# A two-group encoder layer on one core: GpSimd's order in the prompt attention, VectorE's order in the first sample step, and a split final step of the ConvFFN

## The reference, cut to what matters

```python
D_MODEL, SEQ, DEC_SEQ, PAST_LEN = 1024, 1024, 64, 2048      # one prompt, one running stream
SB_HEADS, SB_HEAD_DIM, GM_GROUPS, D_FF = 16, 64, 8, 2816

h = rms_norm(x, g_pre_mix)
u_a, v_a, q, k, v_b = split(h @ w_in)
y_a = gelu(u_a) * (tril(w_s) @ layer_norm(gelu(v_a)) + b_s)          # per group, 128-position chunks
# stick-breaking attention, strictly causal, in 128-query blocks:
z = q k^T / 8
after = exclusive reverse cumsum over keys of log_sigmoid(-z)
y_b = exp(log_sigmoid(z) + after) @ v_b
g_a, g_b = sigmoid(h @ w_gate + b_gate)
x = x + rms_norm((g_a * (y_a @ w_branch_a) + g_b * (y_b @ w_branch_b)) @ w_o, g_post_mix)
up = rms_norm(x, g_pre_ffn) @ w_up                                    # 1024 -> 2 x 2816
conv = b_conv + sum_i w_conv[i] * shifted(up, i)                      # causal, width 3
ff = (gelu(conv_gate) * conv_value) @ w_down
x = x + rms_norm(ff, g_post_ffn)
```

## Time and profile before

| | us |
|---|---|
| median of 3 runs | 2316.68 (2316.09 to 2316.88) |
| the profiled execution | 2319.07 |
| its span in the trace | 2317.3 |
| TensorE busy | 2167.2 (94%) |
| VectorE busy | 1317.6 (57%) |
| GpSimd busy | 921.4 (40%) |
| ScalarE busy | 746.1 (32%) |
| granted TensorE clock, mean | 0.973 |

### The profile page before, as it was taken

One profiled execution on the slowest core, in us unless ns is written; L12 is line 12 of the kernel. 1 busy time (PEld: TensorE's weight loads), 2 busy tenths in 40 slices (PEclk: granted clock), 3 DMA queues, 4 the chain that ended last, 5 costly groups with the idle time before them and its releaser, 6 DMA issues. The chain is left out here.

```text
span 2317.3 us, 33750 instructions
## 1 busy us (share of the span) xinstructions
PE 2167.2 (94%) x12884; PEld 2057.6 (89%) x12884; DVE 1317.6 (57%) x1715; ACT 746.1 (32%) x1435; POOL 921.4 (40%) x495
## 2 busy tenths in 40 slices
PE   6999999998898999989996989799999999999993
PEld 6999999998888999979996968799999999999992
DVE  5044120004777777856554557676776767667666
ACT  3222102225666766744332122212121121211212
POOL 2335334446655555547552210423324233242404
PEclk9999999999999999999997989899999999999996
DMA  5125324636544554565636342201111111111104
GB/s 171 46 78 178 119 76 135 170 125 164 147 113 111 140 131 122 136 186 145 183 105 197 112 163 87 87 28 55 39 43 48 34 54 36 45 45 36 45 0 165
DMA packets 290821, 237.40 MB, mean 102 GB/s; under 512 B 51142, under 2 KB 267926, under 8 KB 290710
## 3 DMA queue, kind: packets, MB, share of 16 engines
q1 hardware_dynamic: 281968, 222.24, 33.2%
q10 hardware_dynamic: 7510, 9.19, 1.3%
q0 software_dynamic: 1232, 4.46, 0.5%
HBM read 168.51 MB, written 67.33 MB: 102 GB/s over the span
## 5 line engine op out<-in xcount | busy, mean ns | idle before, releaser
L1131 DVE TENSOR_TENSOR_SCAN p_rest<-p_rest 128x896 f32<-128x896 f32 (+7 forms) x128 | 230.4, 1814 | 249.6 <-ACT p_rest L1064 249.2
L168 PE MATMUL p_psU<-mergedT_lo,p_w_hi 128*128 128x364 f32 x1056 | 347.0, 329 | 3.3 <-ACTq L2146 3.3
L170 PE MATMUL p_psU<-mergedT_hi,p_w_lo 128*128 128x364 f32 x1056 | 347.7, 329 | 0.0
L169 PE MATMUL p_psU<-mergedT_hi,p_w_hi 128*128 128x364 f32 x1056 | 347.3, 329 | 0.0
L148 POOL TENSOR_SCALAR p_w_hi<-p_w_raw 128x1024 fp32r<-128x1024 f32 x72 | 98.3, 1366 | 558.3 <-PE p_psD L170 417.4
L2169 DVE TENSOR_TENSOR p_acc<-p_psD,p_acc 128x512 f32<-128x512 f32 (+1 forms) x396 | 273.3, 691 | 45.3 <-PE p_psD L170 44.0
L282 PE MATMUL p_psB<-hT_lo,w_hi 128*128 128x364 f32 x888 | 295.6, 333 | 2.4 <-issue 2.4
L282 PE MATMUL p_psB<-hT_hi,w_lo 128*128 128x364 f32 x888 | 293.2, 330 | 0.0
L282 PE MATMUL p_psB<-hT_hi,w_hi 128*128 128x364 f32 x888 | 292.4, 329 | 0.0
L922 POOL TENSOR_TENSOR p_weights<-p_weights,p_rest 128x895 f32<-128x895 f32 (+7 forms) x128 | 171.1, 1348 | 184.2 <-DVE p_rest L1131 184.2
L168 PEld LDWEIGHTS p_psU<-mergedT_lo,p_w_hi 128*128 128x128 f32 x1056 | 199.2, 189 | 5.6 <-POOLq L132 3.4
(11 more groups left out here) (255 smaller groups left out, 4692.7 us busy)
## 6 DMA issues: line engine op xcount, KB each, us to landing
p_w_raw<-in_w_up SPq DMA_DIRECT2D x44, 512.0 KB, 3.7
w_raw<-in_w_in SPq DMA_DIRECT2D x40, 512.0 KB, 3.9
p_w_raw<-in_w_down SPq DMA_DIRECT2D x22, 512.0 KB, 3.5
p_kT<-k_hi_scratch SPq DMA_DIRECT2D x32, 256.0 KB, 4.7
p_kT<-k_lo_scratch SPq DMA_DIRECT2D x32, 256.0 KB, 5.2
w_raw<-in_w_gate SPq DMA_DIRECT2D x16, 512.0 KB, 4.0
p_raw_v<-in_cache_sb_v SPq DMA_DIRECT2D x8, 1024.0 KB, 6.1
p_raw_k<-in_cache_sb_k SPq DMA_DIRECT2D x7, 1024.0 KB, 6.4
```

What stands on the lines that cost most here:

```text
L168: nc.tensor.matmul(out, stat_hi, mov_lo, start=first, stop=False)
L169: nc.tensor.matmul(out, stat_hi, mov_hi, start=False, stop=False)
L170: return nc.tensor.matmul(out, stat_lo, mov_hi, start=False, stop=last)
L1131: nc.vector.tensor_tensor_scan(src, src, src, 1.0, ALU.mult, ALU.bypass).then_inc(s("scanned"), 1)
```

## The change

It has four parts.

1. **Projection's end.** The subtraction of the last line moves from GpSimd to VectorE.
2. **Prompt attention.** `FIRST` goes from 60 to 69. In GpSimd's loop a unit's weight blocks are split behind its weighings, counted one unit further (`blocks_ended(k)` to `blocks_ended(k + 1)`, from 0 for unit 0).
3. **Sample step 0.** VectorE does the keys K1 to K3 ahead of `weigh_low`, and its four y_a rows behind it. SyncE loads the first block of w_branch_a behind y_a row 4, no longer behind row 7.
4. **ConvFFN's end.** The loop runs to step 19. In the last step (`last`) TensorE makes both ups, and then 18 shares of six passes each, three of f = 20 and three of f = 21. The value's convolution goes by chunks of 364. The end goes by groups of three tiles: VectorE adds a tile's shares, makes the rstd of three tiles in one chain (`normalise`, in PSUM but for rstd), and finishes tiles 0 to 5 as they come (`finish`): ScalarE scales them into PSUM (`scaled`), VectorE adds x. Tiles 6 to 8 take VectorE's one instruction as before. GpSimd multiplies all nine by g.

```diff
-                low(NB - 1)
...
+                n, b = NB - 1, (NB - 1) % 2
+                dve.wait_ge(s("hi"), splits_before(n) + 1)
...
+                nc.vector.tensor_tensor(lo[b][:, 0:COLS].bitcast(F32R), line[b][:, 0:COLS], hi[b][:, 0:COLS],
...
-    FIRST, BETWEEN = 60, 48
+    FIRST, BETWEEN = 69, 48
...
                 for k in range(len(UNITS)):
-                    for n in range(blocks_ended(k - 1), blocks_ended(k)):
-                        if n + 2 <= DB:
-                            split(n + 2)
                     for e in range(groups_ended(k - 1) if k else groups_ended(0), min(groups_ended(k), NQ)):
                         q_lo(e)
                     for b in scored(k):
                         weigh(b)
+                    for n in range(blocks_ended(k) if k else 0, blocks_ended(k + 1)):
+                        if n + 2 <= DB:
+                            split(n + 2)
...
                 load_k(1)
-                for j in range(4, KT):
+                load_ya(4)
+                load_w(2)
+                for j in range(5, KT):
                     load_ya(j)
-                load_w(2)
...
                             scan_low(t)
+                        if t == 0:
+                            for n in range(1, 4):
+                                item(t, f"K{n}")
+                        if present(t, "z"):
                             weigh_low(t)
-                    for j in range(passed(i), passed(i + 1)):
-                        if j % 2:
+                    if t == 0 and what == PLAN[-1]:
+                        for j in range(1, KT, 2):
                             ya_lo(j)
...
+                def last(f, b):
+                    up(f, b, 0)
+                    up(f, b, 1)
+                    ring.ready(pe, f * 3 + 2)
+                    pe.wait_ge(s("hid_lo"), f + 1)
+                    for m in range(TILES):
+                        r, c = rows(m), slice(col(m), col(m) + rows(m))
+                        pe.wait_ge(s("last_lo"), HID_NEEDED[m])
+                        for h in range(2):
+                            n = 2 * m + h
+                            pe.wait_ge(s("added"), (f - 1) * SHARES + (n + 1))
...
+                def scaled(m):
+                    r = rows(m)
+                    act.wait_ge(s("rstd"), m // GROUP + 1)
+                    act.wait_ge(s("times_g"), m + 1)
+                    if m:
+                        act.wait_ge(s("finished"), m)
+                    nc.scalar.activation(normed[0:r, :], acc[0:r, m, :], ACT.Copy, scale=rstd[0:r, m:m + 1]).then_inc(s("scaled"), 1)
...
+                for m in range(TILES):
+                    add_share(FT - 2, 0, (m,))
+                    if m % GROUP == 0 and m:
+                        normalise(m // GROUP - 1)
+                    if m > GROUP:
+                        finish(m - GROUP - 1)
+                finish(DIRECT - 1)
+                normalise(TILES // GROUP - 1)
+                for m in range(DIRECT, TILES):
+                    finish(m)
```

More of the change, by code:

```diff
@@ L1663, in _ @@
                 for i, (t, what) in enumerate(FLAT):
[L1664 removed]
+                    if what[0] == "A" and present(t, what) or what[0] == "K" and what != "K0" and present(t, what) and t:
                         item(t, what)
@@ L1989, in phase_ffn @@
     AHEAD = Weights.AHEAD
-    EARLY = 6
+    GROUP = 3
+    DIRECT = TILES - GROUP
+    HID_NEEDED = [max(c for c in range(NCH) if c * CH < col(m) + rows(m)) + 1 for m in range(TILES)]
     with ExitStack() as ctx:
@@ L2023, in bodies, with chunk @@
             step(1, 1, False)
-            with eng.Fori(1, FT // 2) as i:
+            with eng.Fori(1, FT // 2 - 1) as i:
                 step(i * 2, 0, False)
                 step(i * 2 + 1, 1, False)
+            step(FT - 2, 0, False)
             tail(FT - 1, 1)
+        def chunk(c):
+            return slice(GAP if c == 0 else c * CH, (c + 1) * CH)
         with nc.Block() as block:
@@ L2162, in _, with add_share @@
             def _(dve):
-                def add_share(f, b):
-                    for m in range(TILES):
+                def add_share(f, b, tiles=range(TILES)):
+                    for m in tiles:
                         for h in range(2):
```

150 lines of the change are left out of this document (115 added, 35 removed).

## The result

| | before | changed |
|---|---|---|
| median, us | 2316.78 (4 runs) | 2295.57 (4 runs, 2293.62 to 2299.11) |
| ratio | | 0.9911, 95% interval 0.9894 to 0.9928 |
| profiled execution, us | 2319.07 | 2293.94 |
| its span | 2317.3 | 2292.2 |

The changed kernel is 21.2 us faster; forecast were 15.1, and 2295.57 lies in the range of 2290 to 2310. The forecast of 2301.6 was 6 us too high: the term of the ConvFFN's end held, that of the prompt attention had the wrong sign, and that of the sample phase has the right size for reasons that are partly others.

A forecast was written before the change was run, and what follows sets the result against it. TensorE, busy in 94% of the span, was taken as the bound, except at its waits and at the end, which is VectorE's. Terms -20.3 + 4.5 + 1.8 - 1.1 = -15.1 from the median 2316.68 gave 2301.6 us, range 2290 to 2310.

The forecast's parts named there:

- the term of the ConvFFN's end: ConvFFN's end: the 9.44 us wait ahead of the last `down` and its low clock go, VectorE late next; -20.3 us.
- that of the sample phase: Sample step 0: wait for keys goes, but VectorE's late y_a rows delay ScalarE's sigmoid 3.4 us, slow clock 1.1; +4.5 us.
- Rival D: ConvFFN's end: VectorE blocked for the whole of each GpSimd multiplication; +25.8 us in all, 2342; chance 0.02.
- a sign that it is wrong: Sample step 0: wrong if the last y_a row is done before the second half of the values starts.
- then a wait of some 5 us: Sample step 0: TensorE waits some 5 us for ScalarE's sigmoid, with the slow clock, 1.1 us, behind it.
- (a): Projection's end: GpSimd's 2.5 us subtraction takes 1.3 on VectorE, done ahead of TensorE's last matmul; -1.0 us.
- (b) and (c): Prompt attention's start: `FIRST` 69 about even, GpSimd's new unit 0 order delays head 1's turn; +1.8 us including the projection's end.
- (d): Prompt attention, later heads: six blocks end one unit earlier, so splits move and head periods change; -1.1 us.
- x: Prompt attention: period of a head with the split ahead of both weighings, no q subtraction; 27.0 us, between 25.5 and 29.4.
- rival A: Sample step 0 and attention: y_a rows no obstacle, moved splits cost nothing; -25.2 us, 2291.5; chance 0.2.
- C: Sample step 0: change doesn't do what it says but loses nothing, -0.7 there, all else as forecast, 2296.4; chance 0.2.
- The reading of the shared ports: VectorE beside GpSimd: port pair locked for a whole instruction; VectorE instructions with at most one SBUF input need none.

## Why the prediction came out as it did, point by point

**ConvFFN's end: -20.3 forecast, -21.4 measured.** Put on the old scale (+3.73 us, the difference of the phase's starts), the forecast's stations are 2250.7, 2262.6, 2290.5 and the trace's 2250.6, 2263.1 and 2290.0. The chains, finals and the wait for ScalarE (1.34 for 1.4) are as priced. The last final was 0.5 us earlier than forecast, and what follows it took 5.9 and not 6.5. Rival D fell; the kernel with the chain in SBUF lost 7.4 us of the 40.9 that D counted.

**Sample step 0: +4.5 forecast, +4.4 measured in the phase, +3.2 at the last scan (four traces: 3.2, 2.8, and twice 6.4).** That +4.4 meets +4.5 is luck. Engines by turns and a new wait released by a y_a row are as forecast, the terms are not. The forecast has the sigmoid 3.4 us later and 1.1 of low clock. Measured are 1.1 (43.0 us into the phase for 41.9), 2.1 of low clock (1.9 up to the next score, the rest up to the one behind it), and 1.2 behind the last scan, of which the forecast has nothing.

| us from the phase's start | forecast | measured |
|---|---|---|
| raw block of w there | 13.6 | 16.1 |
| VectorE's row 1 done | 35.1 | 32.9 |
| GpSimd's rows 4 and 6 done | 33.9 | 38.8 |
| last of the eight rows done | 45.2 | 42.8 |

The block came 3.0 us earlier than before and not 5.5, so GpSimd was up to 5 us behind its forecast, and the last row was done as the second half of the values began to run. The forecast itself had named that as a sign that it is wrong. In two of the four traces the last row comes behind that half, as forecast; the forecast did not say that the outcome is not one number. The step "then a wait of some 5 us" became two waits, 3.59 and 4.56. And an earlier start of GpSimd is no help by itself: with the old order the load alone costs 3.1.

**Prompt attention, (a): -1.0 forecast.** The gap went from 2.66 to 1.91, which is 0.75 of it. Over all traces the phase begins at 527.8 in the mean of the six without this part and at 526.7 in the eight with it, so -1.1; single traces of one kind lie up to 1.5 apart.

**(b) and (c): +2.8 behind the phase's start forecast, about -1.2 measured.** This step failed, at two places. The forecast waits are there, 4.11 and 2.58. But the late block was done at 565.42 (GpSimd's subtraction starts at 561.77 and takes 3.65) and not "at about 568.8", and "the turn of head 1 at 587.8, not 584.5" did not follow: that turn came at 584.59. From the phase's start this is 1.5 us later than before, which the 1.5 us of dense work done ahead make good, where the forecast had 4.3. GpSimd made up for the late block in its idle time, and its next subtraction took 2.39 and not the 3.97 that it had beside VectorE. The other place: I gave heads 1 and 2 nothing, because no split moves in head 1. In these stretches, before and now,

```profile
576.68:608.00 31.32, 26.05 (x179) 24.88 (x179) 22.90 (x25) 19.69 (x47) 21.73 (x14) 1.00 0.50 129
608.00:637.42 29.42, 26.19 (x180) 25.00 (x180) 21.88 (x24) 18.36 (x44) 15.92 (x11) 1.00 0.64 155
```

```profile
578.62:607.25 28.63, 26.05 (x180) 24.74 (x178) 22.12 (x26) 20.15 (x48) 20.86 (x14) 1.00 0.55 142
607.25:634.78 27.53, 25.84 (x180) 24.81 (x178) 22.14 (x26) 18.42 (x43) 16.18 (x11) 1.00 0.57 142
```

the same work of 26 us takes 4.6 us less: TensorE idles 4.3 us and not 8.5. Its waits add up to this. Before there were two a head for a weighing (1.44 and 1.41, 0.85 and 1.41) and two for VectorE's y sums (2.42 and 0.97). Now there is one a head for a weighing (1.10 and 1.08), and 0.83, 0.66 and 0.60 for the y sums. What set GpSimd and VectorE free for this I can't show; it comes with FIRST alone (28.75 and 27.67 us there), so it isn't unit 0's order.

**(d): -1.1 forecast, -4.5 measured.** The kinds were right, and x was 26.5 for 27.0, which is 1.6 us of the miss, as the three heads were multiplied out. 1.4 more is a head of 28.7 for 30.1, the clock's doing and luck: the forecast had no term for it. The remaining 0.4 is spread over the other heads. Here only sizes were off.

**The sum.** The terms of the attention were too high by 7.5, the others by 2.6 together, against medians that hold 3.9 less than the two traces. That the result lies within the range owes something to luck as well: its lower end comes from rival A, which did not happen. A came nearer on (d) (-5.6 for -4.5 measured, with x = 25.5 where 26.5 was measured), and was wrong on the y_a rows and on (b) and (c). The two traces lie 25.1 apart where A has 25.2, but by other terms. C, at 2296.4 the nearest to the median, was wrong in what is its own: the y_a rows were an obstacle.

**The reading of the shared ports.** The forecast held that a VectorE instruction with at most one SBUF input needs none of them, and found that the rows agree. One of its own rows does not: the 2.26 us step of the old chain has a single input. The choice of PSUM was right all the same, and the last section says what the reading lacked.

## What to carry to other kernels

Where two engines take turns, moving one of them earlier is no gain until the other's next steps have been counted: a load moved forward on a third engine cost 3.1 us here. The operands of a short chain beside GpSimd's work on SBUF are worth moving to PSUM (here 7.4 us, from four steps of three elements that waited). And a change to when units begin is felt where the heavy instructions of a slow engine then fall between the short ones: list them before and after, and time each kind of period once. A term that comes out right is not yet a mechanism that is right: compare the stations on the way, too.

## What the runs showed of the hardware that was not expected

- A VectorE instruction with a single SBUF input of three elements waited for GpSimd, 2.34 us; with its operands in PSUM the same step took 0.17. The Trainium skill, page "SBUF — State Buffer", section "Who interferes with whom", says that an instruction with at most one SBUF input stays clear of GpSimd only outside the modes in which VectorE uses both ports, and that `tensor_scalar` can enter these modes. The forecast had left this exception out. With it page and trace agree, and the 2.26 us of the old chain, also a `TENSOR_SCALAR`, had shown it already. That the step ran in such a mode no trace here shows.
- A wait of 2.8 to 2.9 us (3.4 once) on TensorE at the same place of the same code was followed by the lower clock (0.72 to 0.76 over 6 us) in 34 heads of 47 and not in 13 (1.00), at 1.5 us apiece.
- Two starts that lay 0.1 us apart, in one order or the other, went with 3.1 us and more at the last scan (GpSimd's weighing 0.09 us ahead of VectorE's in one trace, at 1029.93 and 1030.02, and 0.03 us behind it in another).
